# One transformer block pair on one core: the gate stage in a new order, and no low parts on GpSimd after unit 27

## What is computed

```python
x = x + merged @ w_out                                   # units "out"
gate = sigmoid(rms_norm(x, ple_norm_g) @ w_ple_gate)     # units "gate"
x = x + gate * (p @ w_ple)                               # units "ple", "ple2"
x = rms_norm(x, final_g)                                 # end of block 1
proj = rms_norm(x, norm_mix_g_2) @ w_in_2                # block 2: units "qi", "ki", "xc", ...
log_a = -8.0 * r * softplus(-lambda)                     # the recurrence, later in block 2
```

## Time and profile before

| | |
|---|---|
| profiled execution, own time | 807.81 us |
| its span | 806.0 us |
| TensorE busy | 779.3 us (97%) |
| VectorE busy | 535.9 us (66%) |
| ScalarE busy | 393.6 us (49%) |
| GpSimd busy | 271.2 us (34%) |
| mean granted clock of TensorE | 0.987 |

### The profile page before, as it was taken

The page is one execution under the profiler, slowest core; times in us unless marked ns, Lnnn a source line. Parts: engine busy times, 40 slices in busy tenths (PEclk is TensorE's granted clock), DMA queues, the critical chain, the costliest instruction groups (busy, mean ns, idle before and its releaser), DMA issues.

```text
span 806.0 us, 14220 instructions
## 1 busy us (share of the span) xinstructions
PE 779.3 (97%) x5914; PEld 742.4 (92%) x5914; DVE 535.9 (66%) x870; ACT 393.6 (49%) x472; POOL 271.2 (34%) x134
## 2 busy tenths in 40 slices
PE   5999999999999998999999999999999999999996
PEld 4998999999989997899999999999999999999995
DVE  4674693998746658883889866565786555455553
ACT  4634354554654446543464554555436544434342
POOL 2898587976544454343644220000000000000000
PEclk8999999999999999998999999999999999999998
DMA  8765454547535567444445655544645654556521
GB/s 258 236 201 165 125 157 143 165 149 217 183 119 175 190 236 235 133 155 130 138 155 161 203 177 163 159 158 157 205 141 182 232 169 168 185 208 208 164 97 52
DMA packets 120625, 138.15 MB, mean 171 GB/s; under 512 B 6704, under 2 KB 111480, under 8 KB 120569
## 3 DMA queue, kind: packets, MB, share of 16 engines
q1 hardware_dynamic: 120089, 135.78, 52.5%
q0 software_dynamic: 480, 1.57, 0.7%
HBM read 133.15 MB, written 4.19 MB: 170 GB/s over the span
## 4 chain that ended last, share of the span: by engine, by line
PE 81%; DVE 12%; ACT 3%; issue 2%; DMA 1%; POOL 1%; SPq 1%; DVEq 0%; ACTq 0%
PE unit L1406 20%; PE unit L1407 19%; PE unit L1408 19%; PE misc L1779 4%; PE misc L1781 4%; PE misc L1782 4%; DVE misc L895 2%; DVE s_wlo L830 2%; ACT s_whi L499 1%; DVE s_b_lo L1085 1%; PE unit L1441 1%; PE unit L1443 1%; PE unit L1445 1%; DVE s_abc L969 1%; DVE s_a_lo L833 1%
## 5 line engine op out<-in xcount | busy, mean ns | idle before, releaser
L434 POOL TENSOR_TENSOR s_wlo<-s_raw,s_whi 128x1024 fp32r<-128x1024 f32 x86 | 238.3, 2786 | 153.6 <-ACT s_whi L499 153.6
L1406 PE MATMUL unit<-s_a_hi,s_whi 128*128 128x256 f32 x816 | 232.5, 285 | 5.9 <-DVE s_wlo L830 3.2
L1407 PE MATMUL unit<-s_a_lo,s_whi 128*128 128x256 f32 x816 | 231.6, 284 | 0.0
L1408 PE MATMUL unit<-s_a_hi,s_wlo 128*128 128x256 f32 x816 | 231.5, 284 | 0.0
L499 ACT ACTIVATE s_whi<-s_raw 128x2048 fp32r<-128x2048 f32 (+2 forms) x94 | 176.5, 1880 | 64.3 <-PE unit L1408 41.9
L830 DVE TENSOR_TENSOR s_wlo<-s_raw,s_whi 128x1024 fp32r<-128x1024 f32 (+1 forms) x69 | 129.1, 1874 | 79.5 <-ACT s_whi L499 79.3
L1406 PEld LDWEIGHTS unit<-s_a_hi,s_whi 128*128 128x128 f32 x816 | 157.2, 193 | 8.1 <-DVE s_wlo L830 3.7
L1406 PE MATMUL unit<-s_b_hi,s_whi 128*128 128x256 f32 x568 | 164.5, 290 | 0.0
L1407 PE MATMUL unit<-s_b_lo,s_whi 128*128 128x256 f32 x568 | 161.7, 285 | 0.0
L1408 PE MATMUL unit<-s_b_hi,s_wlo 128*128 128x256 f32 x568 | 161.5, 284 | 0.0
L1407 PEld LDWEIGHTS unit<-s_a_lo,s_whi 128*128 128x128 f32 x816 | 157.3, 193 | 0.6
(11 more groups left out here) (301 smaller groups left out, 1131.9 us busy)
## 6 DMA issues: line engine op xcount, KB each, us to landing
s_raw<-in_w_in SPq DMA_DIRECT2D x62, 1024.0 KB, 5.6
s_raw<-in_w_up SPq DMA_DIRECT2D x16, 1024.0 KB, 5.5
s_raw<-in_w_down SPq DMA_DIRECT2D x16, 1024.0 KB, 5.1
s_raw<-in_w_pa SPq DMA_DIRECT2D x6, 1024.0 KB, 5.3
s_raw<-in_w_pb SPq DMA_DIRECT2D x6, 1024.0 KB, 5.3
s_raw<-in_w_out SPq DMA_DIRECT2D x4, 1024.0 KB, 5.2
s_raw<-in_w_ple_gate SPq DMA_DIRECT2D x4, 1024.0 KB, 7.3
s_raw<-in_w_o SPq DMA_DIRECT2D x4, 1024.0 KB, 5.1
```

The source lines that it names most:

```text
L434: gp.tensor_tensor(wlo[:, c % SLOTS, cols], raw[:, c % SLOTS, cols], whi[:, c % SLOTS, cols].bitcast(F32), ALU.subtract).then_inc(Sm["pool ...
L1406: pe.matmul(dst, sh, mh, start=first and k == 0, stop=False)
L1407: pe.matmul(dst, sh, ml, start=False, stop=False)
L1408: ins = pe.matmul(dst, sl, mh, start=False, stop=k == kt - 1)
```

## The change

1. `SHARED_END` goes from 64 to 28. GpSimd forms no low parts after unit 27; the 33 units from 28 to 63 that it shared are VectorE's alone, 2048 words at once.
2. The steps of the logarithm are spread over the out units, in three portions, and ScalarE's Exp for it comes ahead of them. The copy of the bias row (`rv_sb`), which the 3 MB store waits for, comes after the first portion.
3. TensorE's bias product (32x128 by 32x256) comes after the first out unit.
4. In the gate stage `hi` runs a unit further ahead (unit c+3 in place of c+2), `lo(c + 2)` stands ahead of the two steps that add to x, and the low parts of the new tiles one step later.
5. The squares are added up on GpSimd, tiles 0 and 1 plus the later pairs, three adds of 128x512 for each kind, and TensorE has 4 square matmuls in place of 16. They stand between the first six and the last two tiles of qi's two units, which now start on the tiles that have arrived.
6. One root and one reciprocal for the factor of both norms: 1/sqrt(s2 + eps*s1 + eps²), in place of two roots and two reciprocals in a row. The first norm's own factor follows, for `xT`, after qi.

```diff
-SHARED_END = 64
+SHARED_END = 28
@@ GpSimd
-            for c in range(SHARED_END):
+            for c in range(FIRST["gate"] + 1):
...
+            for n in range(1, 4):
+                gp.wait_ge(Sm["sq1_done"], n + 1)
+                if n > 1:
+                    gp.wait_ge(Sm["sq1_summed"], n - 1)
+                gp.tensor_tensor(sq1[:, 0:2, :], sq1[:, 0:2, :], sq1[:, 2 * n:2 * n + 2, :], ALU.add
+                                 ).then_inc(Sm["sq1_summed"], 1)
...
@@ ScalarE, gate stage
+            hi(FIRST["gate"] + 2)
             act.wait_ge(Sm["ms_ready"], 1)
             act.activation(r3_bc[:, :], M[4][:, 0:S], ACT.Sqrt, bias=EPS).then_inc(Sm["r1_std"], 1)
...
-                if j < 3:
-                    hi(c + 2)
+                hi(c + 3)
                 act.wait_ge(Sm["x2_ready"], j + 1)
+                if j < 3:
+                    gated_hi(j)
+                act.activation(sq1[...], xT[...], ACT.Square).then_inc(Sm["sq1_done"], 1)
...
+            gated_hi(3)
             act.wait_ge(Sm["s3_pre"], 1)
-            act.activation(r3_bc[:, :], r8_bc[:, :], ACT.Sqrt, bias=EPS).then_inc(Sm["s3_std"], 1)
+            act.activation(r3_bc[:, :], r8_bc[:, :], ACT.Sqrt).then_inc(Sm["s3_std"], 1)
+            act.activation(r2_bc[:, :], M[4][:, 0:S], ACT.Sqrt, bias=EPS).then_inc(Sm["s2_std"], 1)
@@ VectorE, out stage
+                if j == 0:
+                    log_first()
+                    log_terms(11)
+                    ve.wait_ge(Sm["bias_rows_T"], 1)
+                    ve.tensor_copy(rv_sb[:, 0:S], M[4][:, 0:S]).then_inc(Sm["rv_ready"], 1)
+                    ve.memset(rv_sb[:, S:384], NEG).then_inc(Sm["rv_ready"], 1)
+                elif j == 1:
+                    log_terms(9, 7, 5)
+                elif j == 2:
+                    log_terms(3, 1)
+                    log_last()
@@ VectorE, gate stage
+                if j:
+                    gated_lo(j - 1)
+                lo(c + 2)
                 ve.wait_ge(Sm["gate_sig"], j + 1)
...
-            ve.wait_ge(Sm["s2_std"], 1)
-            link(ve.reciprocal(r2_bc[:, :], r3_bc[:, :]))
-            link(ve.tensor_tensor(r8_bc[:, :], M[0][:, 0:S], r2_bc[:, :], ALU.mult))
-            ve.tensor_tensor(r8_bc[:, :], r8_bc[:, :], r2_bc[:, :], ALU.mult).then_inc(Sm["s3_pre"], 1)
+            ve.wait_ge(Sm["ms2_ready"], 1)
+            link(ve.tensor_scalar(r8_bc[:, :], M[4][:, 0:S], EPS, EPS * EPS, ALU.mult, ALU.add))
+            ve.tensor_tensor(r8_bc[:, :], M[0][:, 0:S], r8_bc[:, :], ALU.add).then_inc(Sm["s3_pre"], 1)
             ve.wait_ge(Sm["s3_std"], 1)
-            link(ve.reciprocal(r_bc[:, :], r3_bc[:, :]))
-            ve.tensor_tensor(r_bc[:, :], r_bc[:, :], r2_bc[:, :], ALU.mult).then_inc(Sm["rb_ready"], 1)
+            ve.reciprocal(r_bc[:, :], r3_bc[:, :]).then_inc(Sm["rb_ready"], 1)
@@ TensorE
+            def mean_squares():
+
+                pe.wait_ge(Sm["r1_std"], 1)
+                pe.wait_ge(Sm["x2_ready"], 1)
+                for dst, sq, summed in ((M[4], sq1, "sq1_summed"), (M[0], sq2, "sq2_summed")):
+                    pe.wait_ge(Sm[summed], 3)
+                    for k in range(2):
+                        ins = pe.matmul(dst[:, 0:S], o1024[:, :], sq[:, k, :], start=k == 0, stop=k == 1)
+                ins.then_inc(Sm["ms2_ready"], 1)
+
+            arriving([FIRST["qi"], FIRST["qi"] + 1], b_hi, b_lo, arrival("b2_hi", "b2_lo"), between=mean_squares)
```

More of the change, by code:

```diff
@@ L1068, in _, with gated_lo @@
             link(ve.reciprocal(r_bc[:, :], r3_bc[:, :]))
+            def gated_lo(j):
+                for k in (2 * j, 2 * j + 1):
+                    ve.wait_ge(Sm["b2_hi"], k + 1)
+                    ve.scalar_tensor_tensor(b_lo[:, k, :], xT[:, k, :], col(fm, k),
+                                            b_hi[:, k, :].bitcast(F32), ALU.mult, ALU.subtract
+                                            ).then_inc(Sm["b2_lo"], 1)
             for j in range(4):
@@ L1203, in _ @@
                 if kind == "qi" and j == 1:
+                    ve.wait_ge(Sm["s2_std"], 1)
+                    link(ve.reciprocal(r2_bc[:, :], r2_bc[:, :]))
                     for k in range(KD):
@@ L1596, in _ @@
             per_layer(FIRST["ple"], 0)
+            arriving([FIRST["out"]], b_hi, b_lo, arrival("mg_hi", "mg_lo", 2))
             pe.wait_ge(Sm["late_loaded"], 16 * 7)
@@ L1600, in _ @@
                       ).then_inc(Sm["bias_rows_T"], 1)
-            arriving([FIRST["out"]], b_hi, b_lo, arrival("mg_hi", "mg_lo", 2))
             for j in range(1, 4):
@@ L1617, in _ @@
                 columns(FIRST["gate"] + j, a_hi, a_lo)
-            pe.wait_ge(Sm["r1_std"], 1)
-            for j in range(4):
+            def mean_squares():
+                pe.wait_ge(Sm["r1_std"], 1)
                 pe.wait_ge(Sm["x2_ready"], 1)
-                pe.wait_ge(Sm["sq12"], j + 1)
-                for dst, sq in ((M[4], sq1), (M[0], sq2)):
-                    for k in (2 * j, 2 * j + 1):
-                        ins = pe.matmul(dst[:, 0:S], o1024[:, :], sq[:, k, :], start=k == 0, stop=k == KD - 1)
-            ins.then_inc(Sm["ms2_ready"], 1)
-            pe.wait_ge(Sm["b2_lo"], KD)
+                for dst, sq, summed in ((M[4], sq1, "sq1_summed"), (M[0], sq2, "sq2_summed")):
[4 more added lines that the diff above has]
+            arriving([FIRST["qi"], FIRST["qi"] + 1], b_hi, b_lo, arrival("b2_hi", "b2_lo"), between=mean_squares)
             halves = [slice(0, DH), slice(DH, 2 * DH)]
@@ L1689, in attention @@
                     values(t - 1)
-            for c in range(FIRST["qi"], FIRST["pc2"]):
+            for c in range(FIRST["ki"], FIRST["pc2"]):
                 kind, j = UNITS[c]
```

75 lines of the change are left out of this document (36 added, 39 removed).

## The result

| | before | after |
|---|---|---|
| median of the runs | 811.19 us (810.04 to 812.32, 4 runs) | 797.13 us (795.35 to 797.52, 4 runs) |
| profiled execution, own time (span) | 807.81 us (806.0) | 796.79 us (795.0) |
| TensorE busy | 779.3 us | 772.8 us |
| VectorE busy | 535.9 us | 542.1 us |
| GpSimd busy | 271.2 us | 175.5 us |

The ratio is 0.9828, 95% interval 0.9804 to 0.9852: 14.1 us faster in the medians, 11.0 us in the profiles. The forecast was 8.9 us and 802.9 us; the result lies in its range of 797.0 to 806.8 by only 0.13 us. Timed again with other kernels beside it, the changed kernel had 798.50 us against 810.18 us, a ratio of 0.9860 (0.9835 to 0.9886). Over both series its 10 runs have a median of 797.5 us; the 50 runs of before that stand beside the experiments have 810.3: 12.8 us.

The account below looks back on a forecast made before the run. TensorE was taken to set the end nearly everywhere, except for waits between ple and qi. qi's end 8.9 us sooner, plus 0.4 at pb, less 0.4 for the clock, gave 798.9 us profiled, 802.9 us median; range 797.0 to 806.8.

Parts of the forecast that it names:

- B: All fits: GpSimd's adds slip into VectorE's gaps, unit 48's load is early; 14.5 us gained, 797.3 us; chance 0.22.
- A: Main case: the lists followed to qi's end, new waits included; 8.9 us gained, 802.9 us; chance 0.47.
- Squares, 5.2 us: TensorE's square matmuls ahead of qi: two groups stay of eight, 5.2 us of its own work goes; called the firmest term.
- new waits: TensorE's waits after unit 48, the last for the final sum: 0.3 + 0.4 + 2.1 + 0.8 = 3.6 us.
- Bias product and log term: TensorE's waits ahead of the bias product (1.2 us with start-up) and ahead of unit 47 (1.9 us) go.
- Low parts on VectorE alone: Units GpSimd shared: low part ready about 1.1 us sooner; frees 0.4 us ahead of pb and part of two gate waits.
- the gate's waits: TensorE's waits ahead of units 47 and 48, 1.9 and 2.4 us: the first goes, the second becomes 2.8 us.
- The turns for j = 2 and 3: Gate stage: two GpSimd adds of 1.3 us each hold up VectorE's turn, 6.5 to 7 us in place of 5.3.
- none at 2.8 between 28 and 63: Sign of being right: VectorE's low parts in units 28 to 63 take 2.29 us, with none at 2.8.
- The clock, -0.4 us: TensorE's wait of 2.8 us at unit 48 can bring the clock down (1.0 to 1.2 us) or not; 0.4 us subtracted.
- pb, 0.4 us: TensorE's wait ahead of pb for the low part of x goes, 0.4 us added to the gain.
- The same difference: Last step, profile to median: the runs' median 811.85 lay 4.0 us above the profiled 807.81, so 798.9 gives 802.9 us.

## Why the prediction was right, and where its size was off

- **The path.** That qi's end sets the gain was right, and the steps to it: the store issued at 290.0 us and landed 12.0 us later (foretold about 290, and 11 to 12), unit 48's high part at 311.75 (foretold 311.7), unit 47 without a wait, a wait of 2.59 us ahead of unit 48 (foretold 2.8) behind its load and the root, x ready at 321.4 and 326.4 us (foretold 321.4 and 326.7). qi's end is 10.5 us sooner than before, foretold 8.9.
- **Which rival.** The time, 797.1 us, is the number of B ("all fits", 797.3), but the trace is A's: B's own sign, unit 48 starting without a wait, did not come. That the result is inside the range is in part luck: the range reached so low for B's sake, and A's number of 802.9 was missed by 5.8 us.
- **Squares, 5.2 us.** 4.5 us by the run that undoes it, so 5.2 is within what the runs can tell. The last sum's 0.8 us under "new waits" is no wait: the first of the two groups runs in it, and the trace has none.
- **Bias product and log term.** 1.2 and 1.9 us stood in the sum for "all fits", not in the forecast, which followed the lists to unit 48. The runs bear out that way of counting: both undone together, nothing is lost. Added up piece by piece they would be 3 us; with both back, waits of 1.1 us come back, and even these cost nothing that can be told.
- **Low parts on VectorE alone.** The forecast gave 0.4 us by name and the rest in part of the gate's waits. By itself this edit is 4.7 us, and 6.5 us in the new order, at least as much as the squares, which the forecast called its firmest term.
- **The turns for j = 2 and 3, the mis-sized term.** "These turns take 6.5 to 7" (x ready at 333.7 and 340.6). Measured: x ready at 331.8 and 338.6, turns of 5.4 and 6.8 us. In the first of them the low part had begun ahead of GpSimd's add and it was the add that waited. The earlier trace rows showed only VectorE held up; GpSimd's 3.4 us in the earlier trace rows showed the other half. So unit 51's low part was ready at 336.9 (foretold 338.7), qi's first six tiles were through at 341.4 (foretold 343.0), and qi's end came 1.6 us sooner, at 346.0 in place of 347.6. The low part at 333.53, 3.38 us, also breaks the sign "none at 2.8 between 28 and 63"; it is the only one.
- **The clock, -0.4 us, and pb, 0.4 us.** The clock stayed at 1.00 behind the wait of 2.6 us: nothing lost. The 0.4 us ahead of pb brought ple's end forward by 0.3 to 0.4 us, but was not a gain of its own on top of qi's end, since unit 48 waited for its load. In the profiles 10.5 us are there at qi's end and 0.5 more behind it: 11.0, where the forecast had 8.9 + 0.4 - 0.4.
- **From the profile to the median, the larger miss.** Of the 5.8 us between 802.9 and 797.1, 2.1 lie in the profile (798.9 against 796.8) and 3.7 in this step. "The same difference" of 4.0 us was added for after, and this failed: it was 0.3 us in the first four runs, and 0.7 over ten. Of the 4.0 us, 2.5 are the distance of before's profile from the median of its 50 runs (810.3), which only says that one of the faster runs was profiled, and 1.5 are that its first three runs, with 811.85, lay above that median. By the medians of all runs the gain is 11.0 + 2.5 - 0.7 = 12.8 us, and the 14.1 us of the first four runs are within their spread. The mean granted clock accounts for little of such distances: over the 50 runs of before it and the time go together only weakly (a correlation of -0.38, where -1 would be full agreement), so why one run is faster than another is open in the main.

Left open: the kernel with VectorE alone is 4.1 us slower than the one with the squares on TensorE (805.67 and 801.59 in one series). Undoing the bias product, the log and the roots cost nothing that the runs can tell (2 us), so what is left by argument is the order of the gate stage and qi's start on the tiles that have come; the two traces have 4.8 and 1.1 us of waits at 240 to 450 us. These two edits weren't tried by themselves, and it stays open why the clock fell at 192 and 240 us in some profiles and not in others. No version with all of its matmuls beat the changed kernel by more than the runs can tell.

## What to carry to other kernels

Follow the edits through the engines' lists to the next thing that is late, and don't add up the waits they remove: here the waits that two edits removed were worth nothing, since the next unit waited for its load, and the two edits even put off the store ahead of that load. An engine that helps with half of a step can cost more than it gives when the two hold each other up and a third waits for the later of the two. When two instructions hold each other up, ask which of them starts first. Do not carry one profile's distance from the median over to another kernel: forecast from profile to profile and give the spread of the runs beside it. And where a row of narrow matmuls stands, look at the clock behind it before you price it by its own time.

## What the runs showed of the hardware

- The clock fell to half with TensorE never idle: 4.00 of 4.00 us busy, with weight loads for 3.98, at 352 to 360 us, within and behind a row of 48 matmuls of 128x8; with 6 of them the clock stayed at 1.00 there. A matmul of 128x8 starts 0.11 us behind the one before it, one of 128x256 0.12 us. The Trainium skill, TensorE: Matmul & The Clock Gate, section Part 1, says that the throttled clock is the default and that activity releases it. These rows show a fall with TensorE never idle, which that sentence does not account for; where they differ, the rows decide.
- An add of two 128x512 inputs on GpSimd took 1.30 us alone and 3.29 us when VectorE's low part had begun first; VectorE's low part took 2.29 us ahead of an add and 3.38 us behind one. Taking 33 low parts off GpSimd gave VectorE 25.6 us back in its other steps.
